# Projection half tiles of the local attention regrouped: two groups of products per head pair turn in place of three

## The chip, the cores and the metric

The kernel runs on one core of a Trainium2 chip. The metric is the device time of one execution in microseconds (us), the median of several runs. The engines work side by side, each through its own list of instructions in order: TensorE (PE, matrix products into PSUM), VectorE (DVE), ScalarE (ACT), GpSimd (POOL) and SyncE (SP, which here only issues transfers). They meet in counting semaphores: `wait_ge(sem(x), n)` holds an engine until counter x has reached n.

## The reference, cut to what matters

Two transformer layers run first; a third block then works on their output. The part of interest is the first branch of that block: windowed attention of 8 heads of 64, taken as 4 head pairs, over 512 positions regrouped into 4 residue classes of 128. Per group of window and dilation `A_GROUPS = ((128, 1), (512, 4), (2048, 16))` there are queries, keys and values:

```
u = h @ w_in                       # projections, 1024 inputs, f32
q, k, v = heads of u (3 groups x 8 heads x 64)
q, k = rope(q, pos), rope(k, pos)  # rotation of halves
s = q @ k.T within the window      # scores
out = softmax(s over the groups' keys) @ v
```

The kernel keeps f32 accuracy in a product by splitting both operands in a high and a low part: three products (high-high, high-low, low-high) for one.

## The kernel before

**The stage.** `pair_pe` (TensorE), `pair_act` (ScalarE) and `pair_dve` (VectorE) run the local attention as 16 turns p, four per head pair (one per residue class). A turn has two heads e = 0, 1. Around the attention work of the turns, TensorE computes the projections that are needed later: those of the next head pair (queries and keys of three groups: 6 tiles j = 0 to 5) and, in the last head pair, those of the next branch. A tile is one output bank of 128 x 512; it is 24 matmuls of 512 columns (8 parts of the 1024 inputs, 3 products each) and is computed as two halves of 12 matmuls, `part` 0 and 1. All 24 tiles of the stage, so 48 halves, use one PSUM bank.

**The slots.** Turn p has three places for such halves on TensorE: slot 3p stands after the transposes of head 0 (`turn(p, 0)`, L658) and ahead of the scores of the next turn (`scores(p + 1)`, L645); slot 3p + 1 stands after `turn(p, 1)` and ahead of the product with the values (`values(p)`, L669); slot 3p + 2 stands after the values and, in turns 3, 7, 11 and 15, after `factor` (L676, the transposes of the inverse softmax sums). `SLOT_A[hp]` names, for the 6 tiles made during head pair hp, the slots of their 12 halves: entry 2j is the slot of tile j's first half, entry 2j + 1 that of its second half.

**What hangs on a slot.** The same table orders the other engines. In ScalarE's list the copy of tile j out of PSUM (`copy_qk`, L1624) stands at the slot of its second half, and after an odd tile `high2` (L1951) rounds two halves of a weight chunk. VectorE rotates tile j (`rope_qk`, L2700, L2702, L2704) at that slot + 2 and splits the weights' low part (`split2`, L2631) at that slot + 1, where it does the slots 3p - 2, 3p - 1 and 3p after the masks and maxima of turn p (L761, L763). SyncE issues four transfers (L1055, `swapped<-qk`) as soon as tile j is copied; they bring the tile with its halves exchanged, which the rotation needs.

**The waits of TensorE.** The first half of a tile waits until the tile before it has been copied (L1447) and until its weights are split. `turn` waits for the exponentials (`p_exp`, L709) of its head and for the copy of the last transposes (L716). `scores(p)` waits for both exponentials of turn p - 1 and, for p = 4, 8, 12, for `roped` (L633): all 6 tiles of the head pair that begins there must be rotated. `values(p)` waits for both copies of the transposed probabilities.

Of the kernel before, what the change touches and what calls it, by code (L numbers as in the profile page):

```python
# [129 lines left out]
def build(nc, A, out, PER):  # L130
# [9 lines left out]
    with ctx:  # L140
# [272 lines left out]
        def a_pairs():  # L413

            pairs = []
            for hp in range(A_HEADS // 2):
                buf = qk[:, hp % 2]
                for r in range(RES):
                    own = slice(r * P, r * P + P)
                    score = [(0, S, lambda lo, b=buf, o=own: (b[lo:lo + 64, 0, o], b[lo:lo + 64, 1, :]))]  # L420
                    for gi in (1, 2):
                        score.append((S + (gi - 1) * P, P,
                                      lambda lo, b=buf, o=own, g=gi: (b[lo:lo + 64, 2 * g, o], b[lo:lo + 64, 2 * g + 1, o])))
                    pv = []
                    for e in range(2):
                        vcol = lambda gi: slice((gi * A_HEADS + 2 * hp + e) * HD, (gi * A_HEADS + 2 * hp + e + 1) * HD)
                        pv.append([av[:, c, vcol(0)] for c in range(RES)] + [av[:, r, vcol(1)], av[:, r, vcol(2)]])
                    pairs.append(Pair(score, win[:, r, :], pv))
            return pairs
# [498 lines left out]
        def tokens(pe, slot, half, K, hi, lo, bank, tiles=(0, 1), c0=0, n=256, ready=None):  # L928

            wh, wl = slot_view(w_hi, slot, K), slot_view(w_lo, slot, K)  # L930
            for j, t in enumerate(tiles):
# [4 lines left out]
            return ins  # L936


        SLOT_A = [(0, 0, 1, 1, 2, 3, 4, 4, 5, 5, 6, 7), range(8, 20), range(20, 32),
                  (32, 33, 34, 35, 36, 37, 39, 40, 42, 43, 45, 46)]  # L940
        UNITS_B = [(k, part) for k in range(2, 16) for part in ((0, 1) if k % 4 < 2 or k == 15 else (None,))]
        SLOTS_B = sorted([0] + [3 * p + 1 for p in range(PAIRS)] + [3 * p + 2 for p in (3, 7, 11)] + [3 * PAIRS - 3])
        STAT_B = (4, 5, 6, 7, T_BANK)
# [2 lines left out]
        def slots(*pairs_):  # L946
            out = defaultdict(list)
            for k, f in pairs_:
                out[k].append(f)
            return out  # L950
# [176 lines left out]
        def _(pe):  # L1127
# [363 lines left out]
            def next_tile(hp, j, part):  # L1491
# [3 lines left out]
            pair_pe(pe, a_pairs(), A_BANKS, 1, prob2, prob2_t, inv_a,  # L1495
                    fill=slots(*[(SLOT_A[hp][2 * j + part], partial(next_tile, hp, j, part))
                                 for hp in range(4) for j in range(6) for part in range(2)]),
# [120 lines left out]
        def _(act):  # L1618
# [368 lines left out]
            for j in range(11):  # L1987
                copy_values(j)
            act.preload_act_table_set("natural_log_exp_and_others")
            pair_act(act, a_pairs(), A_BANKS, prob2, prob2_t, norm_a, between=True, lead=partial(copy_values, 11),  # L1990
                     fill=slots(*[(SLOT_A[hp][2 * j + 1], partial(copy_qk, hp + 1, j) if hp < 3 else partial(copy_b, j))
                                  for hp in range(4) for j in range(6)]))
# [112 lines left out]
        def _(dve):  # L2105
# [605 lines left out]
            for c in range(7, C2_QK + 4):  # L2711
# [5 lines left out]
                     fill=slots((0, partial(split2, C2_QK + 4)),  # L2717
                                *[(SLOT_A[hp][2 * j + 1] + 2, partial(rope_qk, hp + 1, j)) for hp in range(3) for j in range(6)],
                                *[(SLOT_A[hp][2 * j + 1] + 1, partial(split2, C2_QK + 3 * hp + 3 + j // 2 + 2))
                                  for hp in range(4) for j in (1, 3, 5)]))  # L2720
# [174 lines left out]
```

## Time and profile before

| | us |
|---|---|
| median of 3 runs | 1966.15 (1964.77 to 1966.39) |
| the profiled execution's own time | 1966.21 |
| span of its instructions | 1964.4 |
| PE busy | 1941.5 (99%) |
| DVE busy | 1263.2 (64%) |
| ACT busy | 872.6 (44%) |

An engine's busy time is the sum in which at least one of its instructions ran. The times of matmuls overlap by design, so what a group of them costs is read from the start of its first to the start of the first of the next group, not from their durations. The stage of the change lies between 1307 and 1516 us from the span's start.

### The profile page before, as it was taken

Reading aid. Unit: us, or ns where it says so; the run is one execution under the profiler, and the core shown is the slowest. Engines: PE = TensorE matmul, PEld = TensorE weight load, DVE = VectorE, ACT = ScalarE, POOL = GpSimd, SP = SyncE. Lnnn points to the kernel's source line nnn. Section 1 sums busy time; section 2 is a strip of 40 time slices with the busy share of each in tenths; the row PEclk is TensorE's granted clock in tenths of the full one; section 3 lists DMA queues with packets and bytes.
Section 4 is the critical chain, followed back from the end, with each engine's and each line's share of the span. In section 5 each row is a group of like instructions: output and inputs, shape, how many; then the busy total and the mean of one; then the engine's idle time right before and its main releaser. Section 6 shows DMA issues by size and latency. Waiting matters only on the chain.

```text
span 1964.4 us, 30653 instructions
## 1 busy us (share of the span) xinstructions
PE 1941.5 (99%) x11538; PEld 1630.9 (83%) x11538; DVE 1263.2 (64%) x1546; ACT 872.6 (44%) x1277; POOL 29.9 (2%) x60
## 2 busy tenths in 40 slices
PE   7999999999999999999999999999999999999998
PEld 5887888898887897888888888997777777888888
DVE  6866777877645866787887646846664644534435
ACT  5345453344323445453344322334445666544343
POOL 2001000000000001000000000000000000000000
PEclk9999999999999999999999999999999999999999
DMA  7213133333324223133333223523331222232322
GB/s 196 86 40 105 44 107 93 100 102 106 101 76 119 74 56 108 44 107 86 107 86 112 93 94 89 179 76 97 91 113 65 64 82 65 86 118 76 98 88 83
DMA packets 241077, 182.42 MB, mean 93 GB/s; under 512 B 12970, under 2 KB 232360, under 8 KB 240574
## 3 DMA queue, kind: packets, MB, share of 16 engines
q1 hardware_dynamic: 238368, 177.37, 30.4%
q0 software_dynamic: 2160, 2.22, 0.6%
q8 instruction: 76, 1.25, 0.3%
q10 hardware_dynamic: 430, 1.23, 0.2%
q14 instruction: 43, 0.35, 0.1%
HBM read 168.21 MB, written 2.10 MB: 87 GB/s over the span
## 4 chain that ended last, share of the span: by engine, by line
PE 88%; DVE 7%; issue 2%; ACT 1%; DMA 1%; DVEq 0%; SPq 0%; POOL 0%; ACTq 0%
PE ps L882 19%; PE ps L884 19%; PE ps L883 19%; PE ps L1421 4%; PE ps L1419 4%; PE ps L1420 4%; PE ps L669 2%; PE ps L645 2%; PE ps L658 2%; DVE amat L2238 2%; PE ps L1317 1%; PE ps L1319 1%; PE ps L1318 1%; PE ps L521 1%; PE ps L490 1%
## 5 line engine op out<-in xcount | busy, mean ns | idle before, releaser
L882 PE MATMUL ps<-h_hi,w_hi 128*128 128x512 f32 (+1 forms) x1248 | 485.6, 389 | 0.8 <-ACT qk L1624 0.4
L884 PE MATMUL ps<-h_hi,w_lo 128*128 128x512 f32 (+1 forms) x1248 | 475.8, 381 | 0.0
L883 PE MATMUL ps<-h_lo,w_hi 128*128 128x512 f32 (+1 forms) x1248 | 473.6, 379 | 0.0
L2124 DVE TENSOR_TENSOR w_lo<-w_raw,w_hi 128x2048 fp32r<-128x2048 f32 (+3 forms) x110 | 227.0, 2063 | 155.6 <-ACT w_hi L1631 148.6
L882 PEld LDWEIGHTS ps<-h_hi,w_hi 128*128 128x128 f32 x1248 | 234.6, 188 | 51.5 <-issue 7.1
L884 PEld LDWEIGHTS ps<-h_hi,w_lo 128*128 128x128 f32 x1248 | 234.4, 188 | 46.3
L883 PEld LDWEIGHTS ps<-h_lo,w_hi 128*128 128x128 f32 x1248 | 234.6, 188 | 45.0 <-issue 1.9
L1631 ACT ACTIVATE w_hi<-w_raw 128x2048 fp32r<-128x2048 f32 (+3 forms) x108 | 186.7, 1729 | 166.6 <-PE ps L1421 111.9
L2631 DVE TENSOR_TENSOR w_lo<-w_raw,w_hi 128x1024 fp32r<-128x1024 f32 (+1 forms) x118 | 126.5, 1114 | 155.5 <-ACT w_hi L1951 154.7
L882 PE MATMUL ps<-w_hi,h_hi 128*128 128x256 f32 x544 | 152.4, 280 | 0.3 <-DVE h_lo L856 0.2
L883 PE MATMUL ps<-w_lo,h_hi 128*128 128x256 f32 x544 | 150.7, 277 | 0.0
L884 PE MATMUL ps<-w_hi,h_lo 128*128 128x256 f32 x544 | 150.7, 277 | 0.0
L1421 PE MATMUL ps<-hid_hi,w_lo 128*128 128x512 f32 x352 | 138.4, 393 | 0.0
L1419 PE MATMUL ps<-hid_hi,w_hi 128*128 128x512 f32 x352 | 137.6, 391 | 0.8 <-DVE w_lo L2124 0.8
L1420 PE MATMUL ps<-hid_lo,w_hi 128*128 128x512 f32 x352 | 137.4, 390 | 0.0
L1829 ACT ACTIVATE rms_a<-a_pad,g 128x512 f32<-128x512 f32 x44 | 35.9, 816 | 188.7 <-DVE a_pad L2461 96.2
L1951 ACT ACTIVATE w_hi<-w_raw 128x1024 fp32r<-128x1024 f32 (+1 forms) x118 | 108.3, 965 | 4.1 <-issue 2.2
L882 PEld LDWEIGHTS ps<-w_hi,h_hi 128*128 128x128 f32 x544 | 102.5, 188 | 1.9 <-DVE h_lo L856 0.7
L883 PEld LDWEIGHTS ps<-w_lo,h_hi 128*128 128x128 f32 x544 | 102.2, 188 | 0.1
L884 PEld LDWEIGHTS ps<-w_hi,h_lo 128*128 128x128 f32 x544 | 102.1, 188 | 0.0
L2467 DVE SCALAR_TENSOR_TENSOR rms_a<-a_pad,g,rms_a 128x512 f32<-128x512 f32 x88 | 66.2, 752 | 40.5 <-ACT rms_a L1829 31.7
L1419 PEld LDWEIGHTS ps<-hid_hi,w_hi 128*128 128x128 f32 x352 | 66.1, 188 | 15.7 <-issue 1.6
(437 smaller groups left out, 3397.3 us busy)
## 6 DMA issues: line engine op xcount, KB each, us to landing
w_raw<-in_ffn_w_up_dram SPq DMA_DIRECT2D x88, 512.0 KB, 4.6
w_raw<-in_w_in_dram SPq DMA_DIRECT2D x41, 1024.0 KB, 5.4
w_raw<-in_w_in_dram SPq DMA_DIRECT2D x32, 512.0 KB, 5.2
w_raw<-in_ffn_w_down_dram SPq DMA_DIRECT2D x32, 512.0 KB, 4.3
w_raw<-in_w_out_dram SPq DMA_DIRECT2D x12, 1024.0 KB, 5.0
w_raw<-in_ffn_w_down_dram SPq DMA_DIRECT2D x16, 384.0 KB, 3.6
swapped<-qk SPq DMA_DIRECT2D x96, 64.0 KB, 2.0
w_raw<-in_w_mem_kv_dram SPq DMA_DIRECT2D x4, 1024.0 KB, 4.9
```

Source lines behind the costliest of these rows:

```text
L645: ins = pe.matmul(ps[:, b, c:c + n], lhs, rhs, start=first, stop=last)
L882: pe.matmul(dst, lh, rh, start=first and j == 0, stop=False)
L883: pe.matmul(dst, lh, rl, start=False, stop=False)
L884: ins = pe.matmul(dst, ll, rh, start=False, stop=last and j == len(order) - 1)
L1419: pe.matmul(dst, wh[:, k, c], hid_hi[:, h, :], start=h == 0, stop=False)
L1420: pe.matmul(dst, wh[:, k, c], hid_lo[:, h, :], start=False, stop=False)
L1421: ins = pe.matmul(dst, wl[:, k, c], hid_hi[:, h, :], start=False, stop=h == KF - 1)
L1631: act.activation(w_hi[:, slot, 0:n], w_raw[:, slot, 0:n], ACT.Copy).then_inc(sem("w_high"), 1)
L1951: act.activation(w_hi[:, slot, q * n:q * n + n], w_raw[:, slot, q * n:q * n + n], ACT.Copy).then_inc(sem("w_high"), 1)
L2124: dve.tensor_tensor(w_lo[:, slot, 0:n], w_raw[:, slot, 0:n], w_hi[:, slot, 0:n].bitcast(F32), ALU.subtract).then_inc(sem("w_split"), 1)
L2467: dve.scalar_tensor_tensor(conv[:], a_pad[:, slot, w:w + S], g[:, bass.ds(G_CONVW + w * KF + f, 1)], conv[:], ALU.mult, ALU.add).then_inc( ...
L2631: ins = dve.tensor_tensor(w_lo[:, slot, q * n:q * n + n], w_raw[:, slot, q * n:q * n + n], w_hi[:, slot, q * n:q * n + n].bitcast(F32), AL ...
```

## The change

Only the table of slots differs; nothing is computed that was not computed before.

```diff
-        SLOT_A = [(0, 0, 1, 1, 2, 3, 4, 4, 5, 5, 6, 7), range(8, 20), range(20, 32),
-                  (32, 33, 34, 35, 36, 37, 39, 40, 42, 43, 45, 46)]
+        SLOT_A = [(0, 0, 1, 1, 3, 3, 4, 4, 6, 6, 7, 7), (9, 10, 11, 12, 13, 13, 15, 16, 18, 18, 19, 19),
+                  (21, 22, 23, 24, 25, 25, 27, 28, 30, 30, 31, 31), (33, 34, 35, 36, 37, 37, 39, 40, 42, 43, 45, 46)]
```

Slots 3p + 2 are left empty but for 11, 23 and 35, which stand behind `factor` and hold one half each. Counted over the stage, the 48 halves stood in 44 groups and now stand in 35.

TensorE, turn 2 to the scores of turn 4, before. Slot 7 (not shown) precedes the first row; the first rows are `values(2)`; then 12 matmuls of slot 8, of which the first three stand here; the transposes of `turn(3, 0)`; 12 matmuls of slot 9, not shown; and the first matmul of `scores(4)`, which waits for `roped`:

```order
L669 MATMUL ps<-prob2_t_149,av_123 64x128 [waits pt_copied]
L669 MATMUL ps<-prob2_t_149,av_123 64x128 x11
L882 MATMUL ps<-h2_hi_116,w_hi 128x512 [waits tile_copied,w_split]
L883 MATMUL ps<-h2_lo_117,w_hi 128x512
L884 MATMUL ps<-h2_hi_116,w_lo 128x512
...
L658 MATMUL ps<-cm,prob2_148 128x128 [waits pt_copied,p_exp]
L658 MATMUL ps<-cm,prob2_148 128x128 x5
...
L645 MATMUL ps<-qk_132 128x512 [waits p_exp,roped]
```

The same place with the change; both halves of the last tile now stand in slot 7, ahead of the first row:

```order
L669 MATMUL ps<-prob2_t_149,av_123 64x128 [waits pt_copied]
L669 MATMUL ps<-prob2_t_149,av_123 64x128 x11
L658 MATMUL ps<-cm,prob2_148 128x128 [waits pt_copied,p_exp]
L658 MATMUL ps<-cm,prob2_148 128x128 x5
L882 MATMUL ps<-h2_hi_116,w_hi 128x512 [waits tile_copied,w_split]
...
L645 MATMUL ps<-qk_132 128x512 [waits p_exp,roped]
```

The half tile between the values and the next transposes is gone from this place, and `scores(4)` still waits for the rotations. The same happens ahead of `scores(8)` and `scores(12)`.

VectorE, from the maxima of turn 3 to the inverse of the first head pair; the list reads the same before and after, so that the rotation of tile 5 (the last three rows before L770), which `scores(4)` waits for, still follows the rotation of tile 4 and the split:

```order
L763 TENSOR_REDUCE stats<-ps 128x1 [waits masked]
L2700 TENSOR_TENSOR tmp_154<-swapped,a_sin 128x512 [waits swapped2,tile_copied,nmax]
L2702 TENSOR_TENSOR qk<-qk,a_cos 128x512 [waits rope_sin]
L2704 TENSOR_TENSOR qk<-qk,tmp_154 128x512 [waits rope_cos]
L2631 TENSOR_TENSOR w_lo<-w_raw,w_hi 128x1024 [waits w_high,w_split,roped]
L2631 TENSOR_TENSOR w_lo<-w_raw,w_hi 128x1024 [waits w_high]
L2700 TENSOR_TENSOR tmp_154<-swapped,a_sin 128x512 [waits swapped3,tile_copied]
L2702 TENSOR_TENSOR qk<-qk,a_cos 128x512 [waits rope_sin]
L2704 TENSOR_TENSOR qk<-qk,tmp_154 128x512 [waits rope_cos]
L770 RECIPROCAL stats<-stats 128x8 [waits p_exp,roped]
```

Elsewhere VectorE does one split (L2631, after tile 1 of head pairs 1, 2 and 3) one turn later, behind the masks and maxima. On ScalarE the copy of a tile moves with its second half. At the change from turn 3 to turn 4, tile 1 of head pair 1 had its second half in slot 11 and has it in slot 12 now; of ScalarE's difference there stand here the rows that went from that place (-) and those that are there instead (+ and the last row):

```order
-L709 ACTIVATE prob_148,stats<-ps,stats 128x768 [waits nmax,p_exp]
-L723 ACTIVATE norm_a<-ps 128x512 [waits norm_turned,p_exp]
-L1624 ACTIVATE qk<-ps 128x512 [waits tile_done,norm_kept]
-L1951 ACTIVATE w_hi<-w_raw 128x1024 [waits w_loaded0,tile_copied]
-L1951 ACTIVATE w_hi<-w_raw 128x1024
-L716 ACTIVATE prob_t<-ps 128x768 [waits pt_done]
...
+L723 ACTIVATE norm_a<-ps 128x512 [waits norm_turned,p_exp]
+L716 ACTIVATE prob_t<-ps 128x768 [waits pt_done,norm_kept]
 L1624 ACTIVATE qk<-ps 128x512 [waits tile_done,pt_copied]
```

So the tile's copy (L1624) stood between the copy of the turned inverse sums (L723) and that of the transposed probabilities (L716), and stands behind both now. POOL and SP have the same lists.

## Rows read from the trace of the kernel before

**Rows 1.** The page, part 1: busy time, share, instructions.

```profile
PE 1941.5 (99%) x11538; PEld 1630.9 (83%) x11538; DVE 1263.2 (64%) x1546; ACT 872.6 (44%) x1277; POOL 29.9 (2%) x60
```

**Rows 2.** The page, part 4: chain that ended last, by engine.

```profile
PE 88%; DVE 7%; issue 2%; ACT 1%; DMA 1%; DVEq 0%; SPq 0%; POOL 0%; ACTq 0%
```

**Rows 3.** Busy time by stretch, the stage: PE, PEld, DVE, ACT, POOL, clock.

```profile
1307.00:1516.00 209.00, 208.14 (x1351) 161.51 (x1350) 127.96 (x150) 96.69 (x146) 0.00 (x0) 1.00 0.29 79
```

**Rows 4.** Timeline, turns 2 to 4: start, duration, instruction, idle before.

```profile
1352.63 1.53 PE L669 MATMUL ps<-prob_t,av 128*64 128x128 f32 x24
...
1354.09 0.50 PE L882 MATMUL ps<-h_hi,w_hi 128*128 128x512 f32 x1
...
1356.96 0.82 PE L658 MATMUL ps<-cm,prob 128*128 128x128 f32 x6
...
1357.53 0.48 PE L882 MATMUL ps<-h_hi,w_hi 128*128 128x512 f32 x1
...
1359.12 0.69 DVE L2704 TENSOR_TENSOR qk<-qk,tmp 128x512 f32<-128x512 f32 x1
...
1360.47 1.57 PE L645 MATMUL ps<-qk 64*128 64x512 f32 x12
```

**Rows 5.** Timeline, PE, turns 12 and 13, where slot 38 is empty.

```profile
1485.04 1.53 PE L669 MATMUL ps<-prob_t,av 128*64 128x128 f32 x24
1486.50 0.87 PE L658 MATMUL ps<-cm,prob 128*128 128x128 f32 x6
1487.13 0.48 PE L882 MATMUL ps<-h_hi,w_hi 128*128 128x512 f32 x1
```

**Rows 6.** Timeline, PE, turn 0: slot 1 with two halves.

```profile
1315.27 0.48 PE L882 MATMUL ps<-h_hi,w_hi 128*128 128x512 f32 x1
...
1320.95 1.53 PE L669 MATMUL ps<-prob_t,av 128*64 128x128 f32 x24
```

**Rows 7.** Timeline, PE: transposes between tiles at slots 12 and 18.

```profile
1370.26 0.82 PE L658 MATMUL ps<-cm,prob 128*128 128x128 f32 x6
1371.26 0.47 PE L882 MATMUL ps<-h_hi,w_hi 128*128 128x512 f32 x1 [0.18 <-ACT qk L1624]
...
1396.51 0.82 PE L658 MATMUL ps<-cm,prob 128*128 128x128 f32 x6
...
1397.42 0.50 PE L882 MATMUL ps<-h_hi,w_hi 128*128 128x512 f32 x1
```

**Rows 8.** Timeline, turn 1: from tile 3's last product to its rotation.

```profile
1336.61 1.53 PE L669 MATMUL ps<-prob_t,av 128*64 128x128 f32 x24
1336.78 0.60 ACT L1624 ACTIVATE qk<-ps 128x512 f32<-128x512 f32 x1 [3.27 <-PE ps L884]
1337.40 2.41 SPq L1055 DMA_DIRECT2D swapped<-qk  x4
...
1339.32 0.88 ACT L709 ACTIVATE prob<-ps,stats 128x768 f32<-128x768 f32 x1
...
1341.34 0.69 DVE L2700 TENSOR_TENSOR tmp<-swapped,a_sin 128x512 f32<-128x512 f32 x1 [0.38 <-DMA swapped<-qk]
...
1342.79 0.69 DVE L2704 TENSOR_TENSOR qk<-qk,tmp 128x512 f32<-128x512 f32 x1
```

**Rows 9.** Timeline, turns 6 to 8: the last rotation before `scores(8)`.

```profile
1406.24 3.42 SPq L1055 DMA_DIRECT2D swapped<-qk  x4
...
1412.65 0.69 DVE L2704 TENSOR_TENSOR qk<-qk,tmp 128x512 f32<-128x512 f32 x1
...
1413.39 1.57 PE L645 MATMUL ps<-qk 64*128 64x512 f32 x12
```

**Rows 10.** Timeline, turn 3: the first exponential after `scores(4)`.

```profile
1364.20 0.90 ACT L709 ACTIVATE prob<-ps,stats 128x768 f32<-128x768 f32 x1 [0.44 <-DVE stats L763]
```

**Rows 11.** Busy time by stretch, the span's start, columns as in Rows 3.

```profile
12.30:15.50 3.20, 1.59 (x12) 0.93 (x10) 1.99 (x3) 1.75 (x1) 3.20 (x6) 1.00 1.09 364
15.70:22.30 6.60, 4.18 (x10) 3.03 (x11) 6.30 (x7) 6.60 (x13) 4.71 (x7) 0.50 1.11 181
```

## Prediction, made before the changed kernel ran

> **What bounds the kernel now.** The page comes first: its busy times show which engine leaves no room, and TensorE is busy 99% of the span, with VectorE at 64% and ScalarE at 44% [rows 1]. The chain of work that ended last says whether this is the bound too: 88% of it is TensorE [rows 2]. The stage of the change is the same in small: 208.14 of 209.00 us busy, at full clock [rows 3]. So a stage costs what TensorE's groups take from start to start, and another engine matters only where TensorE waits for it. I therefore read the stage in the timeline, group by group, each from its first start to the next group's.
>
> A turn of three groups reads so [rows 4]: from the values (1352.63) 1.46 us to slot 8's products, 2.87 for its 12 matmuls, 0.57 for the transposes, 2.94 for the 12 of slot 9, then the scores. Where the third slot is empty, the values take the same 1.46 and the transposes behind them 0.63 [rows 5]. A slot with two halves takes 5.68 [rows 6].
>
> **First term: merged groups.** The change removes no matmul. Nine groups go (44 to 35), each a half tile between values and transposes. Such a half with the transposes behind it costs 2.87 + 0.57 = 3.44 us. Put beside another half, it costs 5.68 - 2.94 = 2.74, and the transposes, now straight behind the values, 0.63: 3.37. That is 0.07 for each group, 9 x 0.07 = 0.6 us less. The gain is small because changing from products to attention work costs TensorE next to nothing.
>
> **Second term: waits for the copy.** All 24 tiles go through one bank. Where a tile ends in a slot 3p + 2, only the transposes lie between its last product and the next tile's first. They take 0.57, but the copy comes 0.17 after the last product and takes 0.60 [rows 8], so TensorE waits. In slot 18 the products start 0.91 after the transposes instead of 0.57; in slot 12, behind the inverse sums' transposes, 1.00 [rows 7]. There are three places of each kind (slots 6, 18, 30 and 12, 24, 36): 3 x 0.34 + 3 x 0.43 = 2.3 us. With the new table no tile ends in such a slot: the halves kept in 11, 23 and 35 are first halves, and the second needs no copy. Between a tile's end and the next one's start there are now values and transposes (1.46 + 0.63 = 2.09) or scores and transposes (1.57 and more), against the copy's 0.77. All six waits go. Sum so far: -2.9 us.
>
> **Third term: the rotations ahead of a new head pair.** `scores(4)` waits for tile 5 of head pair 1. Its second half stays in slot 7, but slot 8 behind it is emptied, so TensorE reaches the scores sooner after the tile's end. Before, from values(2) to the scores: 1360.47 - 1352.63 = 7.84 us, and the rotation was over at 1359.12 + 0.69 = 1359.81, just 0.66 earlier [rows 4]. Now TensorE needs 1.46 + 0.63 + 2.94 = 5.03.
>
> How fast can the rotation be? Tile 3 shows it undisturbed [rows 8]: from the start of the values (1336.61) copy at 0.17, four transfers from 0.79, the rotation's first operation at 4.73, when VectorE had idled 0.38 for the transfers, and its last ended at 1343.48: 6.87. Tile 5 had the same end before (7.18) with a later split in front. It will now follow tile 3's times: the maxima of turn 3 and the rotation of tile 4 come earlier against tile 5's end by the half that moved ahead of it (2.74), and the split waits for `high2` just as for tile 3. From VectorE's end to the scores' first matmul I take 0.05, which `scores(8)` shows: it started at 1413.39 behind a rotation that ended at 1413.34 [rows 9]. So the wait is 6.87 + 0.05 - 5.03 = 1.89 us, and it stands at `scores(4)`, `scores(8)` and `scores(12)`: 3 x 1.89 = +5.7. The last head pair's tiles are not rotated here. Queued behind the waiting scores are the next transposes and products, so all of TensorE stands still; ScalarE and VectorE soon wait for it too.
>
> What can stretch this term is the issuing of the four transfers: it took 2.41 us for tile 3, 3.42 for tile 5 of head pair 2 [rows 8, 9], so that rotation came 1.0 later. Bounds of a wait: 0 if the rotation came 1.9 earlier, which the serial chain copy, transfers, three operations excludes unless the transfers land faster; 2.9 with late transfers. I take 1.89.
>
> **What I cost at nothing.** Transposes straight after the values need the next exponential. From the scores' start to that exponential's end it takes 1364.20 + 0.90 - 1360.47 = 4.63 [rows 4, 10]; TensorE now comes to those transposes after some 1.57 + 0.63 + 2.94 + 1.46 = 6.6 (1.57 is the scores' busy time), in turns 5 and 9, which have only two halves. Cover left: 1.9. The second exponential, which the next scores need, stands behind `high2` where an odd tile ends: it was over at 1340.20, 3.59 after the values' start [rows 8], and the earliest scores come at 5.03, cover 1.4. The splits moved one turn later are needed a turn or more after that. Weight loads, issued after splits, have the same lead. If one of these covers failed, each turn in question would lose the missing tenths.
>
> **Sum.** -0.6 - 2.3 + 5.7 = +2.8 us. Made against the profiled execution: 1966.21 + 2.8 = 1969.0; that execution is 0.06 above the median shown, so the median becomes 1966.15 + 2.8 = 1969.0 as well, +0.14%. I take 0.2% (3.9 us) as what can be told from no change.
>
> **Rivals.**
> (a) Transfers late at one or more of the three rotations, by 1.0 each as in rows 9: one gives 1970.0, two 1971.0, three 1972.0. For: the SP list is unchanged, and one of the two sets shown was late. Against: the undisturbed one looks regular.
> (b) Faster: the rotations are hidden anyway, no wait at the three scores, and only the first two terms count: 1966.15 - 2.9 = 1963.3. It decides from the point where a rotation ends within 5.0 us of the values' start. Against it: tile 3's 6.87 is a serial chain, copy to 0.77, four issues to 3.2, landing to 4.73, three operations to 6.87, with nothing in it that the change shortens. With the waits cut to a third (0.6 each) it would be 1965.0.
> (c) The six copy waits come back in other places, as a wait of the tile after two halves: -0.6 + 5.7 gives 1971.3. Against: 2.09 against 0.77.
> (d) Exponentials or maxima late in turns with fewer halves, 0.5 in some six turns: +3 more, 1972.0. Against: covers of 1.4 and 1.9.
> (e) The clock. In the stage it is at 1.00, the 2.4 GHz level [rows 3]. At the span's start TensorE was busy 1.59 of 3.20 us, and then ran 6.60 us at 0.50, the 1.2 GHz level [rows 11]. Such a stretch behind each of the three waits would cost up to half of 6.6 us each: 1969.0 + 3 x 3.3 = 1978.9. A wait of 1.9 us between full stretches is far less idle than in that row, so by the row I count nothing. The Trainium skill ("TensorE: Matmul & The Clock Gate", section "HAM oscillation — how this bites in real kernels") says that waits for data between bursts of products can send the clock back to half and that each return is paid again; by that rule the sum would be the 1978.9 of this rival, and the trace so far shows it only at the start.
>
> **How the numbers follow.** Forecast as summed 0.50, with a range of its own of 1968.2 to 1969.9; (a) 0.25, of which one late set 0.16; (b) 0.09; (c) 0.06; (d) 0.06; (e) 0.04. Slower by over 0.2% (above 1970.1) are (c), (d), (e), two or three late sets of (a) and half of the case with one: 0.06 + 0.06 + 0.04 + 0.09 + 0.08 = 0.33. Faster by over 0.2% would need a time under 1962.2; full (b) gives only 1963.3, which is 0.15%, so faster keeps 0.04 for gains not listed. The rest, 0.63, is within 0.2%. The range of 8 in 10 runs from 1966.9 (forecast with waits one third smaller, rounded by the runs' own spread) to 1971.8 (two late sets with the spread): left out are (b), (e) and a part of (a) and (d).
>
> **What the changed profile should show.** Products behind the transposes after 0.57 or 0.63 everywhere, none at 0.91 or 1.00 (second term). The values followed by transposes at 1.46 in turns 0 to 2, 4 to 6 and 8 to 10 (first term). `scores(4)`, `(8)`, `(12)` starting 6.9 us after the values ahead of them, TensorE idle 1.9 before each with the rotation L2704 as the releaser (third term); In the stage TensorE's idle time, now 209.00 - 208.14 = 0.86, grows to between 5 and 6. I am wrong in the third term if these scores start at 5.0, and in the costs set at nothing if TensorE idles before L658 or at other scores. If the clock of the stage is under 1.00, it is (e).

## The result, and the profile after

| | before | after |
|---|---|---|
| median, us (lowest to highest, runs) | 1966.17 (1964.24 to 1969.36, 21) | 1970.04 (1966.78 to 1975.51, 21) |
| ratio, 95% interval | | 1.0022 [1.0016, 1.0028] |
| span of the profiled execution, us | 1964.4 | 1969.2 |
| stage of the change in it, us (below) | 208.68 | 213.54 |

The kernel became slower by 3.9 us, where +2.8 was forecast: inside the range, 1.1 above the forecast, and right at the bound of 0.2% (just under it by the medians, just over it by the ratio). One run of the kernel before, 2402.18 us at a mean clock of 0.752 where its others had 0.997 or more, counts in the median 1966.88 given for some experiments below and in none of the ratios.

The stage is measured here from the first start of L658 in turn 0 to the last start of L676 in turn 15. It takes 213.54 - 208.68 = 4.86 us more, and the span 1969.2 - 1964.4 = 4.8 more. So nothing changed outside it in these two executions. The page after, its busy times and its chain by engine:

```profile
PE 1941.4 (99%) x11538; PEld 1631.6 (83%) x11538; DVE 1263.2 (64%) x1546; ACT 872.6 (44%) x1277; POOL 29.9 (2%) x60
...
PE 87%; DVE 8%; issue 2%; ACT 1%; DMA 1%; SPq 0%; DVEq 0%; ACTq 0%; POOL 0%
```

Beside [rows 1] and [rows 2] TensorE's work is unchanged and VectorE has one per cent more of the chain: a few microseconds in which TensorE waits for VectorE hardly show on a page. Busy time by stretch does show them (columns as in [rows 3]; first the stage, then a stretch of 3.3 us in turn 12):

```profile
1307.00:1520.00 213.00, 206.97 (x1344) 161.53 (x1343) 127.81 (x149) 95.96 (x145) 0.00 (x0) 0.99 0.29 77
...
1467.30:1470.60 3.30, 3.30 (x17) 2.07 (x16) 1.13 (x2) 0.00 (x0) 0.00 (x0) 0.50 1.10 355
```

TensorE idles 213.00 - 206.97 = 6.03 us where it idled 0.86 [rows 3], and the clock is 0.99, since in the second row it is at 0.50. The waits of the stage name one releaser (in total, times, longest):

```profile
PE ps L645 <- DVE qk L2704: 6.0, 3, 2.4
```

The place of [rows 4], from the values of turn 2 to the scores of turn 4, in the timeline after:

```profile
1352.01 1.53 PE L669 MATMUL ps<-prob_t,av 128*64 128x128 f32 x24
...
1352.80 2.41 SPq L1055 DMA_DIRECT2D swapped<-qk  x4
...
1353.47 0.88 PE L658 MATMUL ps<-cm,prob 128*128 128x128 f32 x6
...
1354.10 0.48 PE L882 MATMUL ps<-h_hi,w_hi 128*128 128x512 f32 x1
...
1358.21 0.69 DVE L2704 TENSOR_TENSOR qk<-qk,tmp 128x512 f32<-128x512 f32 x1
...
1358.96 1.57 PE L645 MATMUL ps<-qk 64*128 64x512 f32 x12 [1.85 <-DVE qk L2704]
```

The transposes follow the values after 1.46, the products 0.63 later. The rotation is over 6.89 us behind the values' start (1358.21 + 0.69 - 1352.01), and the scores start 6.95 behind it. Without the wait TensorE would have come at 5.03.

The scores of the other two head pairs, each with the values 6.9 to 7.5 us ahead of them (timeline):

```profile
1405.79 1.53 PE L669 MATMUL ps<-prob_t,av 128*64 128x128 f32 x24
...
1406.59 2.97 SPq L1055 DMA_DIRECT2D swapped<-qk  x4
...
1413.29 1.57 PE L645 MATMUL ps<-qk 64*128 64x512 f32 x12 [2.39 <-DVE qk L2704]
...
1460.12 1.53 PE L669 MATMUL ps<-prob_t,av 128*64 128x128 f32 x24
...
1467.02 2.72 PE L645 MATMUL ps<-qk 64*128 64x512 f32 x12 [1.79 <-DVE qk L2704]
1469.67 1.35 PE L658 MATMUL ps<-cm,prob 128*128 128x128 f32 x6
```

At `scores(8)` the four transfers took 2.97 us to issue instead of 2.41, and the wait grew to 2.46 (7.50 from values to scores, less 5.03; the row's 2.39 is the idle part). Behind the wait of `scores(12)` the clock fell: the scores took 2.65 us to the transposes instead of 1.50, the transposes 1.10 to the products instead of 0.63, together 1.62.

So the account of the profiled stage: counted from start to start the waits add 1.92 + 2.46 + 1.86 = 6.24, the half clock 1.64 (the 1.62 and what lies behind it), and without both the stage would take 213.54 - 6.24 - 1.64 = 205.66, that is 3.02 less than before.

### The profile page after: what moved, and what is told of

Read it like the earlier page. It is cut to its first block, busy times and chain, and to the rows that moved or that the text cites. A ratio compares the mean times of both kernels' runs of the same rounds, so it can differ in the third digit from the quotient of the medians.

```text
span 1969.2 us, 30655 instructions
## 1 busy us (share of the span) xinstructions
PE 1941.4 (99%) x11538; PEld 1631.6 (83%) x11538; DVE 1263.2 (64%) x1546; ACT 872.6 (44%) x1277; POOL 29.9 (2%) x60
## 4 chain that ended last, share of the span: by engine, by line
PE 87%; DVE 8%; issue 2%; ACT 1%; DMA 1%; SPq 0%; DVEq 0%; ACTq 0%; POOL 0%
PE ps L882 19%; PE ps L884 19%; PE ps L883 19%; PE ps L1420 4%; PE ps L1419 4%; PE ps L1421 4%; PE ps L658 2%; PE ps L645 2%; PE ps L669 2%; DVE amat L2238 2%; PE ps L1317 1%; PE ps L1319 1%; PE ps L1318 1%; PE ps L521 1%; PE ps L490 1%
## 5 line engine op out<-in xcount | busy, mean ns | idle before, releaser
L2631 DVE TENSOR_TENSOR w_lo<-w_raw,w_hi 128x1024 fp32r<-128x1024 f32 (+1 forms) x118 | 126.5, 1113 | 159.1 <-ACT w_hi L1951 158.3
```

The source lines that it names most:

```text
L2631: ins = dve.tensor_tensor(w_lo[:, slot, q * n:q * n + n], w_raw[:, slot, q * n:q * n + n], w_hi[:, slot, q * n:q * n + n].bitcast(F32), AL ...
```

## The experiments

Two accounts of what lies above the forecast are tested, named as in the expectations. Theory A: the rotation waits stand as forecast, and the clock falls to half behind some of them. Theory B: the clock has nothing to do with the waits, and late transfers alone make the rest. Under both, the new table without its waits is 2.9 us faster than before. A further rival is VectorE as the true bound of the stage. Theories C, D and E, on what holds the rotation back, belong to the last three kernels and are told in their expectations. Each kernel below is the changed one with the edit shown, unless it is said otherwise; the times of before in brackets are of the same chip.

### The changed kernel again, with more runs

No edit.

> The changed kernel itself once more, for a second profile and for its spread. Theory A (rotation waits plus the clock): three waits of 1.9 to 2.4 us at scores(4), (8) and (12), each about as in the first profile, but the half-clock stretch that stood behind the third one need not come back at the same place: it may be behind another wait, behind none or behind two, 1.6 us each, and single times spread over 3 to 5 us. Median 1969.5 to 1970.5. Theory B (late transfers alone make what lies above 1969.0): the half clock comes back at the same place and the spread comes from the issuing of transfers, so waits of up to 2.9 us are to be seen.

1970.39 us (before 1966.09), ratio 1.0021 [1.0012, 1.0030], 11 runs from 1967.78 to 1976.0. Its profile, the waits of the stage and two stretches behind the first two:

```profile
PE ps L645 <- DVE qk L2704: 5.5, 3, 1.8
```

```profile
1361.70:1365.00 3.30, 3.30 (x16) 2.79 (x13) 2.68 (x3) 1.24 (x2) 0.00 (x0) 0.50 0.05 13
1416.30:1419.60 3.30, 3.30 (x19) 2.57 (x16) 1.38 (x3) 0.00 (x0) 0.00 (x0) 0.50 0.28 74
```

This time no transfers were late, and the clock fell behind two waits instead of one: stage 214.51 = 205.66 + (1.92 + 1.90 + 1.86) + 3.17, so 1.6 for each fall. That is theory A: the fall moves from wait to wait. The runs sort by their mean granted clock: the five at 0.998 have the median 1968.56, which is +2.5 and near the forecast's +2.8, and the five at 0.996 or less lie between 1971.5 and 1976.0. So the forecast was about the kernel with no fall.

### Needless products that fill the waits

Eight products, whose result the next tile overwrites, stand where TensorE waited:

```diff
+                if hp and j == 0 and part == 0:
+                    c, k = t // 2, bank2[t]
+                    split_ready(c)
+                    pe.wait_ge(sem("tile_copied"), upto(pe, "tile_copied", before2[t] + 1))
+                    for _ in range(8):
+                        pe.matmul(ps[:, k, :], slot_view(w_hi, c % 2, KD)[:, 0, 0:P], h2_hi[:, 0, :], start=True, stop=True)
```

> The changed kernel with 8 needless matmuls of 512 columns (their result is overwritten by the tile that follows) ahead of the tile at slots 9, 21 and 33, 8 x 0.229 = 1.83 us, a little less than the wait of 1.89 us that stands there. TensorE is then busy where it waited, and the scores start at the same time as before. Theory A: no half clock in the stage, the median falls to about 1969.0 (1.0 under the changed kernel) and the times spread no more than those of the kernel before. Theory B: late transfers stay late, so the median stays within 0.3 of the changed kernel, near 1970.0.

1970.15 us (before 1966.09), ratio 1.0023 [1.0014, 1.0032]. The filled place in the timeline, from the values to `scores(4)`, and the stage by windows:

```profile
1350.96 1.53 PE L669 MATMUL ps<-prob_t,av 128*64 128x128 f32 x24
...
1353.05 2.09 PE L1498 MATMUL ps<-h_hi,w_hi 128*128 128x512 f32 x8
...
1357.93 1.57 PE L645 MATMUL ps<-qk 64*128 64x512 f32 x12
```

```profile
1307.00:1518.00 211.00, 209.96 (x1363) 164.33 (x1362) 127.82 (x149) 95.20 (x145) 0.00 (x0) 1.00 0.29 78
```

The scores start 6.97 behind the values as in the changed kernel (6.95), with no wait and the stage at full clock; one wait of 1.0 is left at `scores(8)`, where the transfers were late again. The stage takes 212.36, 1.2 less than after and 2.2 less than in the run above, and it is the 205.66 from above plus 1.94, 2.90 and 1.85 by which the three scores start later than 5.03, with nothing left for the clock: in the profile theory A is right. The median did not follow it to the expected 1969.0; it is near the 1970.0 of theory B. Yet it is not the clock that keeps it there: the mean of the runs' granted clocks is 0.9976, against 0.9977 for before, and the late transfers of the profile are worth 1.0. Four of the 11 runs, at a clock of 0.997 to 0.998, took 1971.7 to 1974.2. They stay open (the last section has a candidate), so that filling the waits was not shown to pay in the median.

### More needless products than there is wait

```diff
-                    for _ in range(8):
+                    for _ in range(13):
```

(The diff is against the kernel of the run above.)

> As fill, with 13 needless matmuls in place of 8 at slots 9, 21 and 33: 13 x 0.229 + 0.1 = 3.1 us, more than the wait even with transfers late by 1.0. The scores come 8.1 us after the values, so that neither a rotation nor late transfers nor the clock can show, and 3 x 3.1 us are paid for certain: 1966.1 - 2.9 + 9.2 = 1972.4. If late transfers are what spread fill (1968.7 to 1974.2), the times now lie within 2 us of each other, as those of cover_kept did. If they spread over 5 us again, something else varies that I have not named.

1975.11 us (before 1966.88), ratio 1.0042 [1.0029, 1.0056], five runs from 1972.03 to 1975.47. The expectation missed: the median is 2.7 above its 1972.4, and the runs lie 3.4 apart instead of within 2. The stage takes 214.64 in the profile, where the expectation's terms give 208.68 - 2.9 + 9.2 = 215.0; what is more in this execution stands ahead of the stage, which starts at 1310.09 instead of 1306.73. There the products have a slower rhythm at full clock, which this edit does not touch (last section). So the stage is bound by TensorE again as soon as it has work, and the median can't be read for 2 us here.

### The waiting rotation made longer

```diff
-                dve.tensor_tensor(tmp2[:], swapped[:, (n + 2) % 4], a_sin[:], ALU.mult).then_inc(sem("rope_sin"), tick("rope_sin"))
-                dve.wait_ge(sem("rope_sin"), upto(dve, "rope_sin"))
+                for _ in range(4 if hp and j == 5 else 1):
+                    dve.tensor_tensor(tmp2[:], swapped[:, (n + 2) % 4], a_sin[:], ALU.mult).then_inc(sem("rope_sin"), tick("rope_sin"))
+                    dve.wait_ge(sem("rope_sin"), upto(dve, "rope_sin"))
```

> The changed kernel with the first operation of the last rotation of each of head pairs 1, 2 and 3 done four times in place of once (same result), 3 x 0.73 = 2.2 us more, so that each of the three waits of TensorE is 4.1 us in place of 1.9. By the waits alone 1970.0 + 6.6 = 1976.6. Theory A: the longer idle brings the half clock behind all or nearly all of the three waits, in every profile, so the time is 1977 to 1981 and TensorE's clock in the stage falls below 1.00 at each. Theory B: the clock has nothing to do with the waits, 1976.6 and at most one half-clock stretch at the same place as before.

1981.84 us (before 1966.09), ratio 1.0078 [1.0064, 1.0092], 0.8 above the top of what was expected. The waits, and the clock at each:

```profile
PE ps L645 <- DVE qk L2705: 12.0, 3, 4.0
```

```profile
1362.40:1365.70 3.30, 3.30 (x19) 2.88 (x16) 2.27 (x3) 0.83 (x2) 0.00 (x0) 0.50 0.01 2
1417.00:1423.70 6.70, 4.89 (x20) 3.54 (x21) 4.14 (x7) 0.39 (x1) 0.00 (x0) 0.50 0.19 52
1478.40:1481.70 3.30, 3.30 (x15) 2.69 (x14) 2.82 (x3) 1.38 (x2) 0.00 (x0) 0.50 0.19 59
```

Every wait of 4.0 us met half clock: two had it behind them, and at the second it began 1.9 us before the wait ended and lasted twice as long. The stage, 223.37, is 17.7 over its 205.66: 12.2 of waits from start to start (4.10, 4.08, 4.03), and 5.5 that come with the clock, 1.8 for each fall. The lengthening of the rotation went one for one into the waits, so the scores do hang on it.

### The half tile ahead of the scores kept as cover

Slots 8, 20 and 32 hold the first half of the next head pair again, between the values and the transposes ahead of its scores. Slots 10 and 22 hold two halves, so that of the six tiles that ended in a slot 3p + 2 just the one in slot 35 is left; 44 groups become 38.

```diff
-        SLOT_A = [(0, 0, 1, 1, 3, 3, 4, 4, 6, 6, 7, 7), (9, 10, 11, 12, 13, 13, 15, 16, 18, 18, 19, 19),
-                  (21, 22, 23, 24, 25, 25, 27, 28, 30, 30, 31, 31), (33, 34, 35, 36, 37, 37, 39, 40, 42, 43, 45, 46)]
+        SLOT_A = [(0, 0, 1, 1, 3, 3, 4, 4, 6, 6, 7, 7), (8, 9, 10, 10, 11, 12, 13, 13, 15, 16, 18, 19),
+                  (20, 21, 22, 22, 23, 24, 25, 25, 27, 28, 30, 31), (32, 33, 34, 35, 36, 37, 39, 40, 42, 43, 45, 46)]
```

> The new table with one half tile put back between values and transposes ahead of each new head pair (slots 8, 20, 32), and the halves of the tiles around it arranged so that a tile ends behind the values only once (slot 35). scores(4), (8), (12) then come 7.84 us after the values ahead of them, against rotations of 6.9. Both theories: no wait for a rotation; five of six copy waits gone (3 x 0.34 + 2 x 0.43 = 1.9) and six groups merged (0.4), so 1966.2 - 2.3 = 1963.9, ratio 0.9988. If the copy waits were worth nothing, it would be 1965.8.

1963.51 us (before 1966.09), ratio 0.9986 [0.9976, 0.9995], all 11 runs between 1962.74 and 1965.16. The timeline around `scores(4)`, and the stage:

```profile
1351.22 1.53 PE L669 MATMUL ps<-prob_t,av 128*64 128x128 f32 x24
...
1355.55 0.81 PE L658 MATMUL ps<-cm,prob 128*128 128x128 f32 x6
...
1357.42 0.69 DVE L2704 TENSOR_TENSOR qk<-qk,tmp 128x512 f32<-128x512 f32 x1
...
1359.06 1.57 PE L645 MATMUL ps<-qk 64*128 64x512 f32 x12
```

```profile
1307.00:1512.00 205.00, 204.82 (x1338) 159.85 (x1338) 127.80 (x149) 95.25 (x144) 0.00 (x0) 1.00 0.30 80
```

The rotation is over at 1358.11, 0.95 ahead of scores that no longer wait. Stage 206.31, 2.37 less than before. Run again on another chip:

> cover_kept once more, for its interval: 1963.5, ratio 0.9986, and again times within 2.5 us of each other.

1964.53 us (before 1966.88), ratio 0.9990 [0.9981, 0.9999], stage 206.26. The gain holds; the runs lay 3.7 us apart, where 2.5 was expected.

### One of the three waits

Head pair 1 has the changed kernel's slots, head pairs 2 and 3 those of the kernel above.

```diff
-                  (21, 22, 23, 24, 25, 25, 27, 28, 30, 30, 31, 31), (33, 34, 35, 36, 37, 37, 39, 40, 42, 43, 45, 46)]
+                  (20, 21, 22, 22, 23, 24, 25, 25, 27, 28, 30, 31), (32, 33, 34, 35, 36, 37, 39, 40, 42, 43, 45, 46)]
```

> The table of cover_kept, but with head pair 1's half tiles where the change puts them (slot 8 empty), so that only scores(4) waits for a rotation; scores(8) and (12) keep their cover. If each wait costs its own 1.9: 1963.5 + 1.9, less 0.1 for one merged group = 1965.3, and half a clock fall (1.7 where it comes) on the mean: 1965.3 to 1967. If the waits only cost together (a chain through the stage), it is nearer 1963.5 or 1970.

1966.98 us (before 1966.88), ratio 1.0002 [0.9993, 1.0012]. The waits of the stage:

```profile
PE ps L645 <- DVE qk L2704: 1.9, 1, 1.9
```

One wait, at `scores(4)` alone; stage 208.13 = 206.3 + 1.9 to a tenth, with no fall of the clock behind it. The median lies 2.45 above that of the kernel without waits on the same chip (1964.53), where the wait alone is 1.9. The runs' mean granted clock is 0.9976 against 0.9979, which is about a third of a fall at 0.0009 each (worked out under rival (e) below).

### Two halves together ahead of every head pair

```diff
-        SLOT_A = [(0, 0, 1, 1, 3, 3, 4, 4, 6, 6, 7, 7), (9, 10, 11, 12, 13, 13, 15, 16, 18, 18, 19, 19),
-                  (21, 22, 23, 24, 25, 25, 27, 28, 30, 30, 31, 31), (33, 34, 35, 36, 37, 37, 39, 40, 42, 43, 45, 46)]
+        SLOT_A = [(0, 0, 1, 1, 3, 3, 4, 4, 6, 6, 7, 7), (9, 9, 10, 10, 11, 12, 13, 13, 15, 16, 18, 19),
+                  (21, 21, 22, 22, 23, 24, 25, 25, 27, 28, 30, 31), (33, 33, 34, 35, 36, 37, 39, 40, 42, 43, 45, 46)]
```

> The third slot stays empty (slots 8, 20, 32), as in the change, but the half that stood there goes into slots 9, 21 and 33, beside the one that is there, ahead of the waiting scores: these come 1.46 + 0.63 + 5.69 = 7.8 us after the values. The same wait for the rotation is then covered by moving the half behind the transposes instead of ahead of them: no wait at scores, five of six copy waits and nine groups less: 1966.1 - 1.9 - 0.6 = 1963.6, like cover_kept. Rival: turns 5, 6, 9 and 10 now have two halves, about 10.1 us, against VectorE work of four mask and maxima operations (3.9), two rotations (4.3) and a split (2.4), 10.6; if VectorE falls behind, TensorE waits for exponentials and it is 1965 or more.

1963.79 us (before 1966.88), ratio 0.9988 [0.9979, 0.9997], stage 206.09, no waits. The rotation has no half tile behind the values as cover here; the tile that follows stands whole between the transposes and the scores, 5.69 instead of 2.94 us, and that is enough. VectorE as the stage's bound is out, since it does the same work in 7 us less than in the changed kernel.

### What the rotation's 6.9 us consist of

Three kernels of one run each (before 1965.14, on the same chip), so their profiles are read and not their times. In the first, two of the four exchange transfers are left out from the seventh rotation on; this kernel leaves half of the exchanged rows stale.

```diff
-                for b in range(4):
+                for b in range(4) if n < 6 else (1, 3):
...
-                dve.wait_ge(sem(f"swapped{n % 4}"), 64 * (n // 4 + 1))
+                dve.wait_ge(sem(f"swapped{n % 4}"), sum(64 if m < 6 else 32 for m in range(n % 4, n + 1, 4)))
```

> The changed kernel with two of the four transfers of each tile of head pairs 1, 2 and 3 left out, so half of the exchanged rows are stale; everything else is as in the changed kernel. Issuing takes 1.1 us in place of 2.4, so the last transfer lands 1.2 to 1.3 us sooner. Theory C (the transfers set the rotation, and the split ahead of it is next in line): the rotation can begin when the split ends, 4.35 us after the values' start in place of 4.73, so each wait is 1.5 in place of 1.9, 1.1 us less in the stage. Rival D (the transfers alone): each wait falls by the whole 1.25, to 0.65, 3.8 us less in the stage. Rival E (VectorE's own order sets it): nothing falls.

1965.62 us, stage 209.93. In the timeline:

```profile
1350.13 1.53 PE L669 MATMUL ps<-prob_t,av 128*64 128x128 f32 x24
...
1350.92 1.14 SPq L1055 DMA_DIRECT2D swapped<-qk  x2
...
1352.12 2.36 DVE L2631 TENSOR_TENSOR w_lo<-w_raw,w_hi 128x1024 fp32r<-128x1024 f32 x2 [2.00 <-ACT w_hi L1951]
1354.39 0.69 DVE L2700 TENSOR_TENSOR tmp<-swapped,a_sin 128x512 f32<-128x512 f32 x1
...
1356.58 1.57 PE L645 MATMUL ps<-qk 64*128 64x512 f32 x12 [1.35 <-DVE qk L2704]
```

The transfers are issued 1.27 us sooner, but the scores come only 0.5 sooner (6.45 behind the values), at all three places: the rotation now starts where the split in front of it ends.

In the second the split is also put behind the rotation:

```diff
-                                *[(SLOT_A[hp][2 * j + 1] + 1, partial(split2, C2_QK + 3 * hp + 3 + j // 2 + 2))
+                                *[(SLOT_A[hp][2 * j + 1] + (2 if hp < 3 and j == 5 else 1), partial(split2, C2_QK + 3 * hp + 3 + j // 2 + 2))
```

> As half_transfers (half of the exchanged rows stale), and on VectorE the last rotation of each head pair ahead of the split in place of behind it. Theory C: now the transfers set it again, at 3.5 us after the values' start: rotation over at 5.6, wait 0.65 at each of the three scores, 3.8 us less in the stage than in the changed kernel. Rival E: no fall against half_transfers.

1966.01 us, stage 208.54. In the timeline:

```profile
1352.21 1.53 PE L669 MATMUL ps<-prob_t,av 128*64 128x128 f32 x24
...
1355.75 0.69 DVE L2700 TENSOR_TENSOR tmp<-swapped,a_sin 128x512 f32<-128x512 f32 x1 [3.55 <-DMA swapped<-qk]
...
1357.94 1.57 PE L645 MATMUL ps<-qk 64*128 64x512 f32 x12 [0.63 <-DVE qk L2704]
```

Now the transfers alone hold it, and the scores come 5.73 and 5.65 behind the values; at `scores(8)` they come at 6.58, where the second transfer was issued in its usual time but took 2.92 us to land instead of 2.0. In the third, the split is moved and all four transfers are issued:

> The changed kernel with the last rotation of each head pair ahead of the split on VectorE, all four transfers kept. Theory C: the transfers set it, at 4.73, so each wait stays 1.9 (plus what late transfers add) and the stage stays at 213 us but for clock falls of 1.6. Rival E: the wait falls by up to 2.4.

1971.74 us, stage 214.65, three waits that sum to 5.6, and the clock fell behind two of them. The order alone changes nothing (rival E is out). So the split ends 4.3 us behind the values and the transfers 4.7; shortening one shows the other. None of the six waits in the two kernels with half the transfers (0.6 to 1.5 us) was followed by half clock.

## Why the prediction held, and where it was off

**First term, merged groups, -0.6: right.** Values to transposes 1.46 and transposes to products 0.63 in the rows above, the half tile between them gone.

**Second term, copy waits, -2.3: right.** No products start 0.91 or 1.00 behind transposes any more. Their sizes can be read from two tables in which the third term is absent. With the cover kept, six groups and five copy waits are gone, by the same prices 6 x 0.07 + 3 x 0.34 + 2 x 0.43 = 2.30, and the stage is 2.37 shorter. With two halves ahead it is nine groups and five waits, 2.51, and measured 2.59. For the changed table the prices give 2.94, where the account of its stage needs 3.02: that one was worked out from the others' sum and not run without its waits, but all three agree within 0.1.

**Third term, rotation waits, 3 x 1.89: right in place and releaser, and in size at two of three.** 1.92, 2.46 and 1.86 in one profile, 1.92, 1.90 and 1.86 in the other. The chain copy, transfers, three operations was read correctly from tile 3, and longer or shorter rotations moved the waits as it says. It left out one thing that did no harm: the split in front of tile 5's rotation ends at about the time at which the transfers land, so with fewer transfers the chain would not have shortened by as much as "serial chain" suggests.

**Rival (a), late transfers: real, one of the three.** +0.55 at `scores(8)` in one profile and none in the other, and +0.96 with the waits filled; forecast at 1.0 each, and given 0.25.

**Rival (e), the clock: the step that was mis-sized.** "By the row I count nothing" failed. The row at the span's start was the wrong one to measure by: it had half its time idle over several microseconds, and I took a shorter wait to be harmless. Of the ten waits of 1.8 to 2.5 us in the profiles of kernels with the four transfers (after, again, one wait, order only), five were followed by a stretch at 0.50, the 1.2 GHz level, at 1.6 us each. The eight profiles without a wait of that length (before, the two with needless products, the three runs of kernels without waits, the two with half the transfers) show no half clock between the first 25 us and the last 4.

How often it comes in all runs, their mean granted clocks tell better than ten waits do. A stretch of 3.4 us at half clock lowers the mean over 1969 us by 3.4 x 0.5 / 1969 = 0.0009. The runs of before have 0.9977 on average (53 runs on two chips), those of the changed kernel 0.9970 (32 runs): 0.7 to 0.9 falls in an execution. As a test of this estimate, the kernel with the long waits has 0.9942, so four, and its profile shows half clock for 13.6 us, four stretches of 3.4. The two profiled executions of the changed kernel had one fall and two, with clocks of 0.996 and 0.995, and so were on the slow side of its runs. So the term is about 0.8 x 1.6 = 1.3 us, 2.4 if the profiles' half of the waits were the rule; it is not 0, and neither is it the 3.3 for each wait of the rival.

The Trainium skill ("TensorE: Matmul & The Clock Gate", section "HAM oscillation — how this bites in real kernels") says that data waits between bursts of products send the clock back and that each return costs; the waits of its example are longer than these. The traces agree that a wait can do it: five of these ten, and all three of 4.0 us, where the trace of before showed none. What decides on which side a wait falls stays open; the same kernel had it at one wait in one execution and at two others in the next.

**Costs set at nothing: right.** TensorE waited for no exponential and no split in the stage; the only releaser of its waits is the rotation. Rivals (c) and (d) fell with that and with the second term, (b) with the third.

The sum with what was measured: -3.0 + 5.7 + 1.3 for the clock + the late transfers' share (0.55 in one of two profiles, 0.3) = +4.3, where the medians have +3.9 (21 runs) and +4.3 (11 runs); the profiled execution has +4.9. The stated range held the result, but its upper part was meant for late transfers, and what filled it was more the clock, which had been given 0.04: that much of the hit is luck.

## What to carry to other kernels

Before halves or groups of work are merged, ask what the one that moves was hiding: here a half tile of 2.9 us behind the values hid a rotation that was over just 0.66 us before its reader, and moving it cost more (5.7) than the merging saved (3.0). The same saving is to be had by merging at a place where nothing is due, which gave 2.4 of the 3.0 us, 0.9986 [0.9976, 0.9995] and again 0.9990 [0.9981, 0.9999]. And a wait of about 2 us on TensorE is to be priced above its own length when the engine is otherwise full. Here the three waits cost (3.9 + 3.0) / 3 = 2.3 us each by the medians, 0.4 more than the 1.9 that they last, late transfers included.

## What the runs showed of the hardware

**Half clock behind short waits.** Waits of 0.6 to 1.5 us: 0 of 7. Of 1.8 to 2.5 us: 5 of 10, 1.6 us each; by the mean clocks of all runs it is nearer one in four. Of 4.0 us: 3 of 3, 1.8 us each. In all of them TensorE was full before and behind the wait.

**Two rhythms of the 256-column products at full clock.** In the value projections ahead of the stage the same instructions are spaced differently in two of the 13 profiled executions (two ahead and the overfull kernel). One of TensorE's groups between 1245 and 1305 us (line, engine, operation, names, shapes, count; busy us and mean ns; idle before), before and in the kernel with two halves ahead, which does not touch this part:

```profile
L882 PE MATMUL ps<-w_hi,h_hi 128*128 128x256 f32 x172 | 47.6, 277 | 0.0
```

```profile
L882 PE MATMUL ps<-w_hi,h_hi 128*128 128x256 f32 x166 | 46.7, 282 | 0.0
```

In 60 us there are 172 or 166 of them, and about as many of each of the two other kinds: 113.3 or 117.8 ns from start to start in the rows of single matmuls. It moves the start of the stage from 1306.9 to 1309.3 or, in the overfull kernel, 1310.1. The granted clock of these stretches was full in both. Its cause is open, and it may be what stretched some runs of the two kernels with needless products; only their profiles could tell, and there was one of each.

**Transfer issues that coincide with an instruction fetch.** One issue on SP normally takes 0.59 us. In each set of four that took 2.97 us or more, one of the four took 1.1 to 1.9, and the queue for instructions moved a block at that moment; other issues that overlapped such a block kept their 0.59. After, by queue, 1405 to 1411:

```profile
q8 instruction: 1, 0.02, 1.1%
...
swapped<-qk SPq DMA_DIRECT2D x4, 64.0 KB, 2.5
```

The rotation ahead of `scores(8)` met such a fetch in seven of the ten profiles of kernels with unchanged order and transfers, before among them. The two were seen together; that the fetch is the cause was not tested.
